# Two weight blocks tile by tile at the end of six stages, part of the norm's squares added on GpSimd, and one ring start moved

## The chip, the core and the metric

The kernel runs on one core of a Trainium2 chip. The metric is the device time of one execution in microseconds (us), the median of several runs. TensorE (PE in the rows; its weight loads are PEld) multiplies, VectorE is DVE, ScalarE is ACT, GpSimd is POOL, and SP is the engine whose queue issues most of the DMAs.

## What is computed

A residual stream x of 256 tokens by 1024 features goes through ten sublayers and a last norm. Each sublayer s is

```
h = rmsnorm(x) * g * (1 + scale_s) + shift_s        # over the 1024 features
x = x + gate_s * sublayer_s(h)
```

Sublayers 0, 2, 3 and 5 are dense (swiglu, 2816 wide: `silu(h @ w_gate) * (h @ w_up) @ w_down`), 1 is an SSD mixer, 4 an MLA attention, 6 and 8 are RWKV and pooling mixers, and 7 and 9 are a PEER layer: 128 * 128 experts, for each expert an input row u and an output row v, `sum over chosen e of gate_e * gelu(h . u_e) * v_e`, computed densely with a gate matrix that is zero where an expert isn't chosen. All in float32; each shift, scale and gate comes from a product of a condition with a modulation matrix.

## The kernel before

x lies in SBUF as 8 tiles (features on partitions) of 128 x 256 tokens. All weights come as 957 blocks of 128 x 1024 floats (512 KB), numbered in the order of use (`BASE` gives a stage's first block), through a ring of slots. `ring_plan` gives every block a slot; `CYCLES[first block] = (at, cycle)` says at which place `at` of which cycle of slots a stage starts. The dense stages use `WIDE`, 12 slots; the mixers behind them use only 4. `BEFORE[n]` is the block that had n's slot before. SP's queue issues the loads strictly in order, and waits ahead of each load until `BEFORE[n]` has been used (semaphore `block_used`, counted by TensorE).

A float32 product is made of three fast ones. For each block ScalarE writes a rounded copy into one of four places (`split_hi`, L1227, `weights_hi`; it waits for the load and until the block four back is used) and VectorE the rest in the block's own slot (`split_lo`, L1745). TensorE then runs for each of 8 tiles three matmuls (w hi by h hi, w hi by h lo, w lo by h hi): 24 matmuls a block. In the first parts of a stage (`columns_in_parts`, L590) one block makes one output tile; in the last part of the stages 0, 2, 3, 5, 7 and 9 (`rows_in_parts`, L622, "row stages") one block adds to all 8 output tiles, which lie in the four PSUM banks `acc`, two to a bank. There the second operand is a gate tile, made by ScalarE (`gate_hi`) and VectorE (`gate_lo`) a block or two ahead, and in the last block `acc_done` tells VectorE after tiles 1, 3 and 5 that a pair is complete.

Between two stages:

- VectorE, `residual` (L1737): `split_lo` of the next stage's first block, eight updates of x, `split_lo` of the second
- ScalarE, `norm_squares` (L1211): behind `split_hi` of the next two blocks (three where the stage is in `EARLY`: 1, 3, 4, 6), eight squares into `SQ`; then, when TensorE is ready, the square root (L1213)
- TensorE, `norm_sum` (L556): for each of 8 tiles 2 matmuls with a tile of ones, which the trace shows as 4; it sums over partitions. In `norm_spread` (L566) the root is spread; `open_acc` (L577) puts zeros in the four banks
- VectorE, `normed`: in an `EARLY` stage `split_lo` of the third block, then the root's refinement (L1705 to L1708), eight normed tiles (L1718); in the other stages `split_lo` of the third block now; then the low parts of h (L1752), and the fourth block
- ScalarE, `shift` (L1219): the high parts of h, each behind a normed tile; in stages not in `EARLY` the third `split_hi` comes ahead of it
- TensorE, `front` (L601, L602, L615): the high parts of two blocks paced by `shift`, the third block, and then the products with the low parts of h; the first block is released (`block_used`) in the middle of L615

GpSimd has its own order, one queue: DMAs of modulation weights (`mod_loads`, which wait for x of the stage and for VectorE's products) and of constants, and some adds inside stages 6 and 8.

Of the kernel before, what the change touches and what calls it, by code (L numbers as in the profile page):

```python
# [98 lines left out]
def uv_cycle(l):  # L99
# [5 lines left out]
          BASE["ffn", 1]: (1, WIDE), BASE["ffn", 2]: (0, WIDE), BASE["mla_in"]: (2, range(RING)), BASE["ffn", 3]: (1, WIDE),  # L105
# [131 lines left out]
EARLY = (1, 3, 4, 6)  # L237
BY_ROWS = (0, 2, 3, 5, 7, 9)
COND_ROWS = {0: 1, 1: 2, 3: 3}
# [25 lines left out]
def _consts():  # L265
# [13 lines left out]
    "norm_sq", "norm_pe", "mla_var", "norm_sqrt", "norm_dve", "h_ready", "x_upd",  # L279
# [7 lines left out]
    "rw_w", "rw_zpad", "rw_zeroed", "rw_shift", "rw_lora", "rw_vres", "rw_vresa", "rw_v", "rw_act", "rw_dve",  # L287
# [10 lines left out]
def build(nc, stream, mods, cols_d, consts_d, x_d, pos_d, wuq_d, wukv_d, cond_d, keys_d, pool_d, lora_d, gup_d, vup_d, acts_d, out_d):  # L298
    with ExitStack() as ctx:
# [50 lines left out]
        SQ = AR[:, 120:128, :]  # L350

# [194 lines left out]
        def _(pe):  # L546
# [5 lines left out]
            def norm_sum(s):  # L552
                for d in range(DT):
                    pe.wait_ge(sem["norm_sq"], 8 * s + d + 1)
                    for tt in range(TT):
                        mm = pe.matmul(PS[:, 2, tt * P:(tt + 1) * P], SQ[:, d, tt * P:(tt + 1) * P], ones, start=d == 0 and tt == 0,  # L556
                                       stop=d == DT - 1, skip_group_check=True)
                mm.then_inc(sem["norm_pe"], 1)
# [59 lines left out]
            def rows_in_parts(w, wl, hi, lo, last=False):  # L618

                for d in range(DT):  # L620
                    for lhs, rhs in ((w, hi), (w, lo), (wl, hi)):
                        mm = pe.matmul(acc[:, d, :], lhs[:, d, :], rhs, start=False, stop=False, skip_group_check=True)  # L622
                    if last and d in (1, 3, 5):
                        mm.then_inc(sem["acc_done"], 1)
                mm.then_inc(sem["block_used"], 1)
# [265 lines left out]
            def rwkv(l):  # L891
# [153 lines left out]
                pe.wait_ge(sem["rw_zeroed"], l + 1)  # L1045
# [62 lines left out]
            def peer(l):  # L1108
# [44 lines left out]
                open_acc()  # L1153

                def value(k, i, last=False):
                    w, wl = parts(v0 + k, i)
                    pe.wait_ge(sem["gate_lo"], i * UV_RING + (GATES["uv", l] + k + 1))
                    rows_in_parts(w, wl, gat_hi[:, k % 4, :], gat_lo[:, k % 4, :], last)

                for k in range(UV_RING):  # L1160
                    value(k, 0)
                pe.wait_ge(sem["pe_gelu"], NK * (l + 1))
                rephase(3)
                with pe.Fori(0, NK // UV_RING - 2) as i:
                    for k in range(UV_RING, 2 * UV_RING):
                        value(k, i)
                for k in range(UV_RING, 2 * UV_RING):
# [1344 lines left out]
```

## Time and profile before

| | us |
|---|---|
| median of 3 runs | 3295.07 |
| lowest, highest | 3293.87, 3315.15 |
| profiled execution | 3303.25 |
| its span | 3301.5 |
| PE busy in the span | 3180.2 (96%) |
| VectorE busy | 2521.2 (76%) |
| ScalarE busy | 1603.3 (49%) |
| GpSimd busy | 197.1 (6%) |

Times in rows are us from the span's start. Matmuls are pipelined: one is shown as about 0.28 long while the next starts 0.113 later. A duration with a count behind it (x8) is that of the whole group from first start to last end. `[0.78 <-PE psum L622]` means that the engine was idle 0.78 us ahead of it and what ended the wait.

### The profile page before, as it was taken

How to read it: one execution, taken by the hardware profiler on the slowest of the kernel's cores; microseconds unless marked ns; L12 is line 12 of the kernel's file. 1: busy time of each engine (PE TensorE's matmuls, PEld its weight loads, DVE VectorE, ACT ScalarE, POOL GpSimd, SP SyncE). 2: the span in 40 equal slices, each digit the busy share in tenths (PEclk: the TensorE clock that was granted, in tenths of full speed). 3: DMA queues.
4: the chain of work that ended last, by engine and by line, in shares of the span. 5: the costliest groups of instructions: out<-in, count | busy, mean ns of one | idle time of the engine just before them, and what ended most of it. 6: DMA issues, size and time to landing. Idle time of an engine off the chain costs nothing.

```text
span 3301.5 us, 71408 instructions
## 1 busy us (share of the span) xinstructions
PE 3180.2 (96%) x28256; PEld 3061.2 (93%) x28256; DVE 2521.2 (76%) x4560; ACT 1603.3 (49%) x2581; POOL 197.1 (6%) x331
## 2 busy tenths in 40 slices
PE   6999989999999999899999999999899999999998
PEld 6999769999967998889999999998789999999998
DVE  7989657989835896748978877776756978867776
ACT  4466644454544445335455454444425455554444
POOL 1100001111100110200000000000400000000000
PEclk9999999999999999999999999999899999999999
DMA  9965218979721993146875477774226885567774
GB/s 394 382 234 167 77 39 317 387 293 387 278 83 51 402 363 119 47 164 211 241 216 170 145 262 235 236 234 156 84 98 196 243 234 174 174 210 235 236 234 161
DMA packets 246741, 707.37 MB, mean 214 GB/s; under 512 B 27488, under 2 KB 93024, under 8 KB 245456
## 3 DMA queue, kind: packets, MB, share of 16 engines
q1 hardware_dynamic: 212256, 572.17, 52.0%
q0 software_dynamic: 34224, 131.55, 10.5%
q8 instruction: 185, 3.03, 0.4%
q14 instruction: 76, 0.62, 0.1%
HBM read 669.00 MB, written 34.60 MB: 213 GB/s over the span
## 4 chain that ended last, share of the span: by engine, by line
PE 89%; DVE 5%; DMA 3%; ACT 2%; issue 1%; SPq 0%; POOL 0%; DVEq 0%; ACTq 0%; POOLq 0%
PE psum L590 40%; PE psum L622 29%; PE psum L1149 3%; PE psum L1081 1%; PE psum L721 1%; DMA ring<-stream 1%; PE psum L973 1%; PE psum L556 1%; PE psum L996 1%; PE psum L769 1%; PE psum L601 1%; DVE ring L1745 1%; PE psum L602 1%; PE psum L888 1%; DVE arena L1803 1%
## 5 line engine op out<-in xcount | busy, mean ns | idle before, releaser
L590 PE MATMUL psum<-hh,weights_hi 128*128 128x256 f32 x4216 | 1186.7, 281 | 19.2 <-ACT arena L1444 8.8
L590 PE MATMUL psum<-h,weights_hi 128*128 128x256 f32 x4216 | 1171.6, 278 | 0.0
L590 PEld LDWEIGHTS psum<-hh,weights_hi 128*128 128x128 f32 x4216 | 798.0, 189 | 25.5 <-issue 11.3
L590 PEld LDWEIGHTS psum<-h,weights_hi 128*128 128x128 f32 x4216 | 797.4, 189 | 0.2
L622 PE MATMUL psum<-small,weights_hi 128*128 128x256 f32 x2752 | 768.1, 279 | 4.5 <-DVE ring L1745 3.9
L622 PE MATMUL psum<-work,weights_hi 128*128 128x256 f32 x2752 | 766.5, 279 | 0.0
L1745 DVE TENSOR_TENSOR ring<-ring,weights_hi 128x1024 fp32r<-128x1024 f32 x463 | 566.0, 1225 | 181.7 <-ACT weights_hi L1227 176.9
L1227 ACT ACTIVATE weights_hi<-ring 128x1024 fp32r<-128x1024 f32 x463 | 488.2, 1056 | 374.0 <-PE psum L622 182.0
L590 PE MATMUL psum<-hh,ring 128*128 128x256 f32 x2016 | 562.4, 279 | 0.0
L622 PEld LDWEIGHTS psum<-small,weights_hi 128*128 128x128 f32 x2752 | 519.4, 189 | 5.5 <-DVE ring L1745 5.4
L622 PEld LDWEIGHTS psum<-work,weights_hi 128*128 128x128 f32 x2752 | 519.0, 189 | 0.0
L1227 ACT ACTIVATE weights_hi<-arena 128x1024 fp32r<-128x1024 f32 x334 | 351.5, 1053 | 100.0 <-PE psum L590 78.7
L590 PEld LDWEIGHTS psum<-hh,ring 128*128 128x128 f32 x2016 | 383.2, 190 | 0.0
L622 PE MATMUL psum<-small,ring 128*128 128x256 f32 x1280 | 354.0, 277 | 0.0
L590 PE MATMUL psum<-hh,more_lo 128*128 128x256 f32 x1240 | 343.7, 277 | 0.0
L1745 DVE TENSOR_TENSOR more_lo<-arena,weights_hi 128x1024 fp32r<-128x1024 f32 x214 | 261.1, 1222 | 52.7 <-ACT weights_hi L1227 48.6
L1657 DVE SCALAR_TENSOR_TENSOR arena<-arena 128x1024 f32<-128x1024 f32 x232 | 282.2, 1219 | 17.8 <-DMA arena<-stream 12.6
L2216 DVE TENSOR_TENSOR work<-work,arena 128x256 f32<-128x256 f32 x256 | 163.8, 641 | 164.7 <-PE psum L622 164.2
L622 PE MATMUL psum<-small,v_lo 128*128 128x256 f32 x1024 | 289.2, 282 | 0.0
L1566 ACT ACTIVATE small<-psum 128x256 f32<-128x256 f32 x256 | 97.9, 383 | 381.7 <-PE psum L590 376.1
L590 PE MATMUL psum<-hh,u_lo 128*128 128x256 f32 x960 | 265.2, 276 | 0.0
L622 PEld LDWEIGHTS psum<-small,ring 128*128 128x128 f32 x1280 | 240.3, 188 | 0.0
(420 smaller groups left out, 4901.9 us busy)
## 6 DMA issues: line engine op xcount, KB each, us to landing
ring<-stream SPq DMA_DIRECT2D x487, 512.0 KB, 4.2
arena<-stream SPq DMA_DIRECT2D x342, 512.0 KB, 5.2
arena<-mod_weights POOLq DMA_DIRECT2D x224, 512.0 KB, 7.1
v_raw<-stream SPq DMA_DIRECT2D x128, 512.0 KB, 4.4
acts<-small SPq DMA_DIRECT2D x256, 128.0 KB, 3.6
work<-acts SPq DMA_DIRECT2D x256, 128.0 KB, 3.2
arena<-w_uq POOLq DMA_DIRECT2D x1, 3072.0 KB, 10.6
arena<-cond_rows POOLq DMA_DIRECT2D x2, 1024.0 KB, 8.4
```

The lines of the kernel that those rows point to most:

```text
L556: mm = pe.matmul(PS[:, 2, tt * P:(tt + 1) * P], SQ[:, d, tt * P:(tt + 1) * P], ones, start=d == 0 and tt == 0, stop=d == DT - 1, skip_grou ...
L590: mm = pe.matmul(out, lhs[:, d, :], rhs[:, d, :], start=(d == 0 and p == 0), stop=(d == DT - 1 and p == 2))
L601: pe.matmul(out, w[:, d, :], h_hi[:, d, :], start=opens and d == 0, stop=False, skip_group_check=True)
L602: pe.matmul(out, wl[:, d, :], h_hi[:, d, :], start=False, stop=False, skip_group_check=True)
L622: mm = pe.matmul(acc[:, d, :], lhs[:, d, :], rhs, start=False, stop=False, skip_group_check=True)
L721: mm = pe.matmul(to, XTOK[:, tt, at], rhs, start=k == 0, stop=k == 3, skip_group_check=True)
L1149: mm = pe.matmul(PS[:, 4 + g % 4, j * P:(j + 1) * P], OHI[:, g % 2, j, :], OHJ[:, g % 2, j, :], start=True, stop=True)
L1227: act.activation(whi[:, NTH[n] % WS, :], raw(n), ACT.Copy).then_inc(sem["block_hi"], 1)
L1566: act.activation((rs, rv)[n % 2], PS[:, n % 4, 0:T], ACT.Gelu).then_inc(sem["pe_gelu"], 1)
L1657: return dve.scalar_tensor_tensor(PRODUCT[:, m % 2, :], block, 1.0, COND[:, 0 if g < 6 else 1, :], ALU.mult, ALU.mult, accum_out=modc[:, g ...
L1745: dve.tensor_tensor(low(n), raw(n), whi[:, NTH[n] % WS, :].bitcast(F32), ALU.subtract)\
L2216: dve.tensor_tensor(gat[:, k % 4, :], sil[:, k % 4, :], WALL[:, :, i * UV_RING + k], ALU.mult).then_inc(sem["pe_gated"], 1)
```

## The change

- `last_rows`: in a row stage TensorE runs the last two blocks together, tile by tile: 3 matmuls of the one and 3 of the other for tile 0, and so on. `acc_done` comes after tiles 1, 3, 5 and 6; both blocks are released at tile 7.
- Tile 7 of the row stages is accumulated in bank 0, `PS[:, 0, 0:T]`, opened by a matmul of zeros (`open_last`) behind the column part.
- In dense stages gate tiles use four places instead of two and are made one block further ahead.
- For s in 1, 3, 4, 6, 8 and the last norm GpSimd adds squares 0 to 3 into the place of square 3 (`norm_presum`), and TensorE sums tiles 4, 3, 5, 6, 7 only.
- `EARLY` is gone: in all stages the third block is split behind the squares.
- `CYCLES` of the dense stage 3 (blocks 213 to 278) starts at 6 instead of 0.
- `rw_zpad` is merged into `rw_zeroed`.

The diff, cut to its core:

```diff
-          BASE["ffn", 1]: (1, WIDE), BASE["ffn", 2]: (0, WIDE), BASE["mla_in"]: (2, range(RING)), BASE["ffn", 3]: (1, WIDE),
+          BASE["ffn", 1]: (1, WIDE), BASE["ffn", 2]: (6, WIDE), BASE["mla_in"]: (2, range(RING)), BASE["ffn", 3]: (1, WIDE),
...
-EARLY = (1, 3, 4, 6)
 BY_ROWS = (0, 2, 3, 5, 7, 9)
+PRE, PRESUMMED = 4, tuple(s + 1 for s in BY_ROWS)
...
+        def row_acc(d):
+            return acc[:, d, :] if d < DT - 1 else PS[:, 0, 0:T]
...
             def norm_sum(s):
-                for d in range(DT):
-                    pe.wait_ge(sem["norm_sq"], 8 * s + d + 1)
+                added = s in PRESUMMED
+                order = (PRE, PRE - 1, *range(PRE + 1, DT)) if added else range(DT)
+                for n, d in enumerate(order):
+                    if added and d == PRE - 1:
+                        pe.wait_ge(sem["norm_pre"], (PRE - 1) * (PRESUMMED.index(s) + 1))
+                    else:
+                        pe.wait_ge(sem["norm_sq"], 8 * s + d + 1)
...
+            def last_rows(blocks):
+
+                for d in range(DT):
+                    for block in blocks:
+                        mm = row_parts(d, *block)
+                        if d == DT - 1:
+                            mm.then_inc(sem["block_used"], 1)
+                    if d in (1, 3, 5, 6):
                         mm.then_inc(sem["acc_done"], 1)
+            def open_last():
+
+                pe.matmul(row_acc(DT - 1), zeros[:, :], rep(zeros[:, :], 2), start=True, stop=False, skip_group_check=True)
...
+                pe.wait_ge(sem["ffn_a"], FT * f + FT - 1)
+                open_last()
+                last = []
                 for j in range(FT):
                     w, wl = parts(base + 2 * FT + j)
                     pe.wait_ge(sem["gate_lo"], GATES["ffn", f] + j + 1)
-                    rows_in_parts(w, wl, gat_hi[:, j % 2, :], gat_lo[:, j % 4, :], j == FT - 1)
+                    if j < FT - 2:
+                        rows_in_parts(w, wl, gat_hi[:, j % 4, :], gat_lo[:, j % 4, :])
+                    else:
+                        last.append((w, wl, gat_hi[:, j % 4, :], gat_lo[:, j % 4, :]))
+                last_rows(last)
...
                 root_table((0, 2, 3, 5)[f] + 1)
-                for j in range(FT - 2):
+                gate_hi(2)
+                for j in range(FT - 3):
                     ready(base + 2 * FT + j)
-                    gate_hi(j + 2)
+                    gate_hi(j + 3)
...
-                    for p in range(3 if s in EARLY else 2):
+                    for p in range(2):
                         split_hi(FIRST[s] + p)
                 norm_squares(s)
-                if s and s not in EARLY:
+                if s:
                     split_hi(FIRST[s] + 2)
...
-                    if s in BY_ROWS and d < 6:
-                        dve.wait_ge(sem["acc_done"], 3 * BY_ROWS.index(s) + d // 2 + 1)
+                    if s in BY_ROWS and d < 7:
+                        dve.wait_ge(sem["acc_done"], 4 * BY_ROWS.index(s) + d // 2 + 1)
...
+            def norm_presum(s):
+
+                for d in range(1, PRE):
+                    pool.wait_ge(sem["norm_sq"], 8 * s + d + 1)
+                    if d > 1:
+                        pool.wait_ge(sem["norm_pre"], (PRE - 1) * PRESUMMED.index(s) + d - 1)
+                    pool.tensor_tensor(SQ[:, d, :], SQ[:, d - 1, :], SQ[:, d, :], ALU.add).then_inc(sem["norm_pre"], 1)
```

VectorE's gates in the dense stages are moved in the same way as ScalarE's, the PEER stages call `last_rows` for their last two blocks, and `norm_presum` stands in GpSimd's queue behind the modulation loads of the stage ahead (stages 1, 3, 4), ahead of the constants of stages 6 and 8, and at the end for the last norm.

## Rows read from the trace of the kernel before

**Rows 1.** The page, part 4: the chain that ended last, by line.

```profile
PE psum L590 40%; PE psum L622 29%; PE psum L1149 3%; PE psum L1081 1%; PE psum L721 1%; DMA ring<-stream 1%; PE psum L973 1%; PE psum L556 1%; PE psum L996 1%; PE psum L769 1%; PE psum L601 1%; DVE ring L1745 1%; PE psum L602 1%; PE psum L888 1%; DVE arena L1803 1%
```

**Rows 2.** Chain of stage 0's end (start us, us, what).

```profile
204.93 14.39 PE psum L622 x127
219.32 3.58 PE psum L556 x32
```

**Rows 3.** Timeline behind stage 0 (start, us, engine, line, tiles, count [idle <-releaser]).

```profile
217.32 3.23 DVE L1737 SCALAR_TENSOR_TENSOR x<-psum,modc,x 128x256 f32<-128x256 f32 x8 [0.78 <-PE psum L622]
217.84 3.16 ACT L1211 ACTIVATE arena<-x 128x256 f32<-128x256 f32 x8
...
222.62 0.64 PEld L577 LDWEIGHTS psum<-zeros 128*128 128x128 bf16 x4
222.93 0.26 ACT L1213 ACTIVATE small<-psum,eps 128x2 f32<-128x2 f32 x1 [1.93 <-PE psum L556]
224.78 3.22 DVE L1718 SCALAR_TENSOR_TENSOR h<-x,modc,psum 128x256 f32<-128x256 f32 x8 [0.81 <-PE psum L566]
...
232.52 0.47 ACT L1282 ACTIVATE arena<-psum,cols 128x256 f32<-128x256 f32 x1 [2.97 <-PE psum L615]
```

**Rows 4.** Timeline, stages 6 and 8: GpSimd adds and VectorE beside them.

```profile
1310.93 2.47 POOL L2320 TENSOR_TENSOR arena<-arena 128x1024 f32<-128x1024 f32 x1 [40.66 <-DVE arena L1981]
1311.19 2.48 DVE L1974 SCALAR_TENSOR_TENSOR arena<-arena,cols 128x256 f32<-128x256 f32 x1
1315.64 0.48 DVE L1974 SCALAR_TENSOR_TENSOR arena<-arena,cols 128x256 f32<-128x256 f32 x1
...
2371.05 0.73 POOL L2355 TENSOR_TENSOR small<-small,arena 128x256 f32<-128x256 f32 x1
2371.46 0.41 DVE L2023 TENSOR_TENSOR arena<-psum,arena 128x256 f32<-128x256 f32 x1
```

**Rows 5.** Timeline, ScalarE and VectorE behind stage 7.

```profile
2273.87 1.05 ACT L1227 ACTIVATE weights_hi<-ring 128x1024 fp32r<-128x1024 f32 x1
2275.56 3.22 DVE L1718 SCALAR_TENSOR_TENSOR h<-x,modc,psum 128x256 f32<-128x256 f32 x8 [0.81 <-PE psum L566]
2278.70 1.22 DVE L1745 TENSOR_TENSOR ring<-ring,weights_hi 128x1024 fp32r<-128x1024 f32 x1
...
2283.62 0.39 ACT L1444 ACTIVATE arena<-psum 128x256 f32<-128x256 f32 x1 [3.29 <-PE psum L615]
```

**Rows 6.** Timeline, TensorE behind stage 9.

```profile
3288.41 3.73 PE L556 MATMUL psum<-kept,arena 128*128 128x128 f32 x32
```

**Rows 7.** Chain from stage 3 into stage 4.

```profile
896.76 3.24 DVE x L1737 x8
...
904.49 12.32 DMA arena<-constants
```

**Rows 8.** Timeline in stage 8: SP issues a lone load, ScalarE takes it.

```profile
2283.55 13.88 SPq L536 DMA_DIRECT2D ring<-stream  x6
...
2286.89 1.06 ACT L1227 ACTIVATE weights_hi<-ring 128x1024 fp32r<-128x1024 f32 x1 [2.88 <-DMA ring<-stream]
```

**Rows 9.** The page, part 6 (queue, operation, count, KB each, us to landing).

```profile
ring<-stream SPq DMA_DIRECT2D x487, 512.0 KB, 4.2
```

**Rows 10.** Chain behind stage 2.

```profile
711.95 3.58 PE psum L556 x32
715.56 0.27 ACT small L1213
```

**Rows 11.** TensorE by stretch (us, busy (x count), granted clock, DMA share, GB/s).

```profile
376.00:378.00 2.00, 0.00 (x0) 1.00 0.70 236
378.00:380.00 2.00, 0.00 (x0) 0.62 0.07 27
...
386.00:388.00 2.00, 2.00 (x7) 0.50 0.00 0
388.00:390.00 2.00, 2.00 (x11) 0.82 0.00 0
```

More of the change, by code:

```diff
@@ L552, in norm_sum @@
             def norm_sum(s):
[L553 to L554 removed]
+                added = s in PRESUMMED
[5 more added lines that the diff above has]
+                        pe.wait_ge(sem["norm_sq"], 8 * s + d + 1)
                     for tt in range(TT):
[L556 removed]
+                        mm = pe.matmul(PS[:, 2, tt * P:(tt + 1) * P], SQ[:, d, tt * P:(tt + 1) * P], ones, start=n == 0 and tt == 0,
                                        stop=d == DT - 1, skip_group_check=True)
@@ L616, in front, with row_parts, rows_in_parts @@
                     mm.then_inc(sem["block_used"], 1)
-            def rows_in_parts(w, wl, hi, lo, last=False):
-                for d in range(DT):
-                    for lhs, rhs in ((w, hi), (w, lo), (wl, hi)):
-                        mm = pe.matmul(acc[:, d, :], lhs[:, d, :], rhs, start=False, stop=False, skip_group_check=True)
-                    if last and d in (1, 3, 5):
+            def row_parts(d, w, wl, hi, lo):
+                for lhs, rhs in ((w, hi), (w, lo), (wl, hi)):
+                    mm = pe.matmul(row_acc(d), lhs[:, d, :], rhs, start=False, stop=False, skip_group_check=True)
+                return mm
+            def rows_in_parts(w, wl, hi, lo):
+                for d in range(DT):
+                    mm = row_parts(d, w, wl, hi, lo)
+                mm.then_inc(sem["block_used"], 1)
[4 more added lines that the diff above has]
+                        if d == DT - 1:
+                            mm.then_inc(sem["block_used"], 1)
+                    if d in (1, 3, 5, 6):
                         mm.then_inc(sem["acc_done"], 1)
-                mm.then_inc(sem["block_used"], 1)
+            def open_last():
+                pe.matmul(row_acc(DT - 1), zeros[:, :], rep(zeros[:, :], 2), start=True, stop=False, skip_group_check=True)
             def ffn(s, f):
@@ L1165, in peer @@
                     for k in range(UV_RING, 2 * UV_RING):
-                        value(k, i)
-                for k in range(UV_RING, 2 * UV_RING):
-                    value(k, NK // UV_RING - 2, k == 2 * UV_RING - 1)
+                        rows_in_parts(*value(k, i))
+                for k in range(UV_RING, 2 * UV_RING - 2):
+                    rows_in_parts(*value(k, NK // UV_RING - 2))
+                last_rows([value(k, NK // UV_RING - 2) for k in (2 * UV_RING - 2, 2 * UV_RING - 1)])
             def begin(s):
@@ L1720, in normed @@
                 if s in IN_PARTS:
-                    if s and s not in EARLY:
+                    if s:
                         split_lo(FIRST[s] + 2)
@@ L1784, in ffn @@
                         products(2 * k + 1)
-                for j in range(FT - 2):
-                    gate_lo(j + 2)
-                    if j + 4 + 2 * FT < 3 * FT:
+                gate_lo(2)
+                for j in range(FT - 3):
+                    gate_lo(j + 3)
+                    if j + 4 < FT:
                         split_lo(base + 2 * FT + j + 4)
```

37 lines of the change are left out of this document (21 added, 16 removed).

## The prediction

> **What bounds the kernel now.** I read the page first, its chain of work that ended last [rows 1]: two lines, both TensorE's streams of 24 matmuls for one weight block, hold 69% of the span. So the kernel is a train of matmuls, and what the change can touch is what stands between two trains: the norm ahead of each stage. Next I read the chain at the end of stage 0 [rows 2]: 127 matmuls in 14.39 us (0.113 each) run up to 219.32, and then the 32 matmuls of the norm's sum take 3.58 us (0.112 each) without a gap. ScalarE and VectorE beside them [rows 3]: the eight residual updates run from 217.32 to 220.55 (first to last 0.396 apart, each 0.48), the eight squares from 217.84 to 221.00. The last square is done before TensorE comes to it at about 222.3, so it is TensorE, not the residual, that decides when the square root starts (222.93). What the reader is to see: the residual is late but not on the path; the norm's sum is.
>
> **What is added up and left out of the sum.** Four tiles of squares become one. TensorE then does 5 tiles of 4 matmuls instead of 8, so 12 fewer, 12 x 0.112 = 1.34 us per transition [rows 2]. Conditions: the last square and the GpSimd sum must be there. With two blocks interleaved, the train of 48 matmuls starts at 219.32 - 48 x 0.113 - 0.17 = 213.7, and a pair of accumulators is done every 1.36 us, more than the 0.79 us that two residuals take. So only tile 7 is left at the end: residual at 219.36 to 219.84, square to 220.3 [rows 3], ahead of its turn on TensorE (219.3 + 16 x 0.112 = 221.1). GpSimd: tiles 2 and 3 are updated at about 217.5, the square of 3 is there at 217.95. An add of this shape takes 0.73 us [rows 4], and the third ends at about 219.1, some 0.6 us before TensorE has done with tile 4. Hidden, with little to spare.
>
> An add beside VectorE needs a look [rows 4]. A GpSimd add of 2.47 us stretched a VectorE instruction with both inputs in SBUF from the 0.48 us that it takes at 1315.64 to 2.48 us, till after the add had ended (1313.40); an instruction with one input in PSUM kept its 0.41 us beside another add. The residuals read PSUM, so they should keep their time; the split of the second weight block (1.2 us, both inputs in SBUF) starts at 219.85, after the adds. The cost is taken as 0; bounds 0 and one add (0.7 us) per transition. By the Trainium skill, GPSIMD Engine Reference, section Specifications, GpSimd's interfaces to SBUF are shared with VectorE and contend with its instructions that have two SBUF inputs. The trace agrees (2.48 beside 0.48); if that rule bit at each transition it would be the third rival below.
>
> **The split of the third weight block moves.** For stages 1, 3, 4 and 6 it moves from ahead of the squares to behind the square root on ScalarE, and on VectorE from ahead of the root to behind the eight normed tiles. It has to: its place in weights_hi is held by the last block but one, now in use up to the end. The kernel already has this order in stage 8 [rows 5]: ScalarE's 1.05 us (2273.87 to 2274.92) ends before the first normed tile is there (2276.04), free; VectorE's 1.2 us pushes the low parts of h. From the start of the normed tiles to the first evacuation it takes 2283.62 - 2275.56 = 8.06 us there, and 232.52 - 224.78 = 7.74 in stage 1 [rows 3]. So +0.32 us in each of the four. The matmul wait for the low parts is where it sits.
>
> **Stage by stage.** Into stage 1: -1.34 + 0.32 = -1.02. Into 6: the same, -1.02 (the fourth block behind it is fetched by a load that starts when the first is released, so it moves along). Into 8: -1.34, no split moved. Into the last norm: -1.34; the sum follows the matmuls there too, 3.73 us for the 32 [rows 6]. Into stage 4 the chain is another [rows 7]: eight residuals, then GpSimd issues loads that wait for them, and the DMA of 12.32 us up to 916.81 holds the stage. TensorE's gain is lost in that wait; what counts is when the last residual ends, 220.55 - 219.84 = 0.71 us earlier as worked out for stage 0. So -0.71. The turned ring also brings this stage's first loads earlier, but they are not on this path. Sum of the five: -5.43.
>
> The extra matmul that opens the eighth accumulator: four of twice its width load in 0.64 us [rows 3], so about 0.1 us each, six times, on TensorE's path: +0.6. Its waits (for a gate product or gelu two or more blocks back) are over by then; bounds 0 and 1.2. The two gate tiles that must be ready one block sooner are covered by making the third one ahead of the loop; the waits behind which they queue are for block j, as before. On GpSimd the adds are queued ahead of loads that wait for the whole of x, which comes after them, so they delay nothing, but in stage 3 perhaps 0.4 us. The merged semaphore costs nothing.
>
> **The ring that was turned.** This is the edit that I would watch. The stage ahead (147 to 212, starting at 1) leaves its last block, 212, in slot (1 + 65) mod 12 = 6. Starting stage 3 at 6 puts its *first* block, 213, in slot 6 as well. SP's queue therefore waits for block 212 to be used before it may load 213, and all later loads queue behind it. Before, the block ahead in that slot was seven blocks back. After 212 is used, in order: the load, ScalarE's rounding, VectorE's low part, and only then the residuals, because both engines have this split queued ahead of the residual and the squares. Prices: a load with nothing else in flight took 2286.89 - 2283.55 = 3.34 us until ScalarE had it [rows 8]; the median over all loads of this kind is 4.2 [rows 9]. The train of stage 2 ends at 711.95 and the square root behind it is at 715.56 [rows 10]. In the new kernel:
> - 711.95 + 0.1 + 3.34 = 715.4 landed; rounding 1.05, 716.45; low part 1.2, 717.7
> - eight residuals 3.23, 720.95; last square 721.4; third add about 721.35
> - TensorE does tile 4 at 720.3, then 16 matmuls from 721.4. At 0.112 that is 1.8 us and the square root starts at 723.4, +7.8 us.
>
> But TensorE has then been idle from 711.95 to 720.3. In a gap that has no matmul from 376 to 380 the granted clock fell from 1.00 (0.62 is a mean over a stretch of both levels); it was 0.50 at 386 to 388, with TensorE at work again, and came back between 388 and 390 [rows 11]. 0.50 is the lower of its two levels, 1.2 against 2.4 GHz. At double the time the 16 matmuls take 3.6 us: +9.6, the value that I take, since the gap here is twice as long as those 4 us. By the Trainium skill, TensorE: Matmul & The Clock Gate, section What's actually happening, the gate knows only these two rates and falls to the lower one when the engine idles. The trace agrees (1.00, 0.50); at the high rate the stage would cost 7.8. With 0.3 for the moved split: +9.9. Bounds: 8.1 (clock kept) and 12.5 (a load of 4.2 us, and a further 1.7 us for matmuls of the front at the lower clock).
>
> **Sum.** -5.4 + 0.6 + 9.9 = +5.1 us on a profiled execution of 3303.25 us (span 3301.5). That one is 8.2 above the median of the runs, 3295.07. The difference carries over: 3295.07 + 5.1 = 3300.2.
>
> **Rivals.**
> - *The turned ring costs nothing* (the load is hidden in some way that I don't see). For it: loads are early in most of the span. Against it: one in-order queue and a wait on block 212. Then -5.4 + 0.6 + 0.3 - 1.34 = -5.8, 3289.2, faster. It decides if the load of 213 is issued before the last matmul of 212. Chance 0.10.
> - *The stall is dearer*: twelve loads are now issued at one go, the first lands at 4.2 us or later, and the half clock lasts into the front. +2.6 to +5: 3303 to 3305. Chance 0.20.
> - *The adds come too late or hold VectorE up.* If the third add ends 1.3 us after 219.1, or two adds hold VectorE's split, each of five transitions loses what it gained: 5.4 less gain, 3305.6. For it: the margin is 0.6 us and [rows 4]. Against: PSUM operands escape. Chance 0.10.
> - Something that I haven't seen makes it slower by over 33 us: 0.02; faster by as much: 0.01.
>
> **How the numbers follow.** The forecast has 0.57, with its own range 3297 to 3303 (the bounds of the stall and of the opening matmul). The range that holds the time 8 times in 10 reaches from the first rival to beyond the third: 3290 to 3307. One per cent is 33 us, about what a measurement of this kernel can tell from no change. All cases but the last lie within it: faster 0.01, same 0.97, slower 0.02.
>
> **What the profile would show.** Right: 20 matmuls of the norm's sum instead of 32 at six transitions, square root 1.3 us after where the train would put it; last residual alone at the end of a row stage; the first evacuation 8.06 us behind the first normed tile everywhere; behind block 212 TensorE idle for about 8 us with ScalarE's wait put down to the DMA of the ring, and a granted clock of 0.50 there. Wrong: a gap of less than 5 us at stage 3; a wait of TensorE on GpSimd in the norm's sum; residuals longer than 0.48 us; or a gain into stage 4 of more than 0.7, if its loads were held up by those that the turned ring moves.

## The result and the profile after

| us | before | after |
|---|---|---|
| median of 20 runs each | 3297.38 | 3309.32 |
| lowest, highest | 3291.95, 3315.15 | 3300.72, 3319.83 |
| profiled execution | 3303.25 | 3304.77 |
| its span | 3301.5 | 3303.1 |

Time after over time before is 1.0031, with a 95% interval of 1.002 to 1.0041: 10.2 us slower (6.6 to 13.5). That is within 1%, as forecast, and on the side that was forecast, but 3309.32 lies 9.1 us above the forecast of 3300.2 and 2.3 above the range. (Each of the kernels e5 and h1 below has one run far from all others, at 8143.96 and 5934.33 us, which neither its median nor its ratio takes in.)

The page of the kernel after: its head, and the chain that ended last by line.

```profile
span 3303.1 us, 71272 instructions
PE 3170.0 (96%) x28190; PEld 3048.8 (92%) x28190; DVE 2520.3 (76%) x4560; ACT 1603.9 (49%) x2581; POOL 212.3 (6%) x349
...
PE psum L599 39%; PE psum L630 29%; PE psum L1182 3%; PE psum L1114 1%; PE psum L754 1%; DMA ring<-stream 1%; PE psum L1006 1%; PE psum L1029 1%; PE psum L610 1%; PE psum L565 1%; PE psum L802 1%; DVE ring L1780 1%; PE psum L611 1%; DVE arena L1839 1%; PE psum L838 1%
```

The two trains hold 68% of the span (L599 and L630 are what L590 and L622 were in [rows 1]). GpSimd has 15 us more to do: 18 adds. Line numbers have moved, so here is the key: L630 is the row train, L565 the norm's sum, L586 the zeros, L575 the spread, L1263 and L1780 the two splits of a weight block, L1247 the squares, L1249 the square root, L1753 the normed tiles, L1772 the residual, L2309 the new GpSimd adds, L540 SP's load.

**The end of stage 0**, chain (start, us, what) and then timeline of the kernel after, to be laid beside [rows 2, 3]:

```profile
204.89 14.85 PE psum L630 x131
219.74 2.24 PE psum L565 x20
222.01 0.27 ACT small L1249
```

```profile
218.42 1.84 DVE L1772 SCALAR_TENSOR_TENSOR x<-psum,modc,x 128x256 f32<-128x256 f32 x4 [0.48 <-PE psum L630]
218.07 1.62 POOL L2309 TENSOR_TENSOR arena<-arena 128x256 f32<-128x256 f32 x2 [0.23 <-ACT arena L1247]
223.86 3.22 DVE L1753 SCALAR_TENSOR_TENSOR h<-x,modc,psum 128x256 f32<-128x256 f32 x8 [0.81 <-PE psum L575]
231.86 0.48 ACT L1319 ACTIVATE arena<-psum,cols 128x256 f32<-128x256 f32 x1 [3.23 <-PE psum L624]
```

What the reader is to see: 20 matmuls in 2.24 us where there were 32 in 3.58, without a gap; GpSimd is done at 219.69, before TensorE comes to the sum's second tile, the one that holds the adds' result (the two rows of VectorE and GpSimd are the last four of eight updates and the last two of three adds). From the last matmul of the train to the first normed tile it takes 223.86 - 219.74 = 4.12 us, and 224.78 - 219.32 = 5.46 before: exactly the 1.34 us forecast.

**The end of stage 2**, chain of the kernel after, to be laid beside [rows 10]:

```profile
699.89 10.55 PE psum L630 x93
710.46 3.55 DMA arena<-stream
714.04 1.06 ACT weights_hi L1263
715.13 1.23 DVE more_lo L1780
716.35 0.41 DVE x L1772
716.78 0.82 ACT arena L1247 x2
717.67 0.73 POOL arena L2309
718.54 0.74 POOL arena L2309
719.40 1.80 POOL arena L2309
721.25 3.80 PE psum L565 x16
725.08 0.27 ACT small L1249
```

Here the train is over at 710.44 and TensorE waits. The load of block 213 starts when block 212 is released, and behind it stand, one after the other, the two splits, one residual, two squares, the adds. Between the train's end and the first normed tile (726.92) lie 16.49 us, where it was 5.46.

The same distance for all kernels below is the table that the rest rests on; what each kernel is follows in the next section. The last column is stage 4 whole, from the last matmul of stage 3's train to the last of stage 4's. Into stages 2, 5, 7 and 9 it is 5.46 in all kernels (once 5.79).

| last matmul to first normed tile, us, into | 1 | 3 | 4 | 6 | 8 | last norm | stage 4 whole |
|---|---|---|---|---|---|---|---|
| before | 5.46 | 5.46 | 6.48 | 5.46 | 5.46 | 5.46 | 170.8 |
| before, a second profile (b1) | 5.46 | 5.46 | 6.57 | 5.46 | 5.46 | 5.46 | 171.1 |
| after | 4.12 | 16.49 | 4.11 | 4.12 | 4.11 | 4.12 | 170.8 |
| after again (e0) | 4.12 | 16.29 | 4.12 | 4.12 | 4.12 | 4.12 | 171.0 |
| after, ring start 0 (e1) | 4.11 | 4.12 | 8.45 | 4.12 | 4.12 | 4.12 | 172.2 |
| before, ring start 6 (e2) | 5.46 | 15.32 | 5.46 | 5.46 | 5.45 | 5.46 | 171.3 |
| after, ring start 2 (e3) | 4.12 | 4.12 | 4.12 | 4.12 | 4.12 | 4.12 | 171.3 |
| e3 again (e4) | 4.12 | 4.12 | 4.11 | 4.12 | 4.12 | 4.12 | 170.2 |
| e3 a third time (e5) | 4.12 | 4.11 | 4.11 | 4.12 | 4.11 | 4.11 | 171.3 |
| e3 without the adds (f1) | 5.46 | 5.46 | 5.46 | 5.46 | 5.45 | 5.46 | 170.1 |
| e3, blocks in turn (f2) | 6.93 | 6.93 | 8.05 | 8.05 | 8.32 | 5.78 | 172.6 |
| e3, one bank less (f3) | 4.12 | 4.12 | 4.12 | 4.12 | 4.12 | 4.12 | 172.3 |
| after, splits behind squares (g1) | 4.12 | 7.24 | 4.12 | 4.12 | 4.12 | 4.12 | 171.1 |
| e3, positions apart (h1) | 4.12 | 4.12 | 4.12 | 4.12 | 4.12 | 4.12 | 168.3 |

### The profile page after: what moved, and what is told of

Its sections match the earlier page's. It is cut to its first block, busy times and chain, and to the rows that moved or that the text cites. A ratio compares the mean times of both kernels' runs of the same rounds, so it can differ in the third digit from the quotient of the medians.

```text
span 3303.1 us, 71272 instructions
## 1 busy us (share of the span) xinstructions
PE 3170.0 (96%) x28190; PEld 3048.8 (92%) x28190; DVE 2520.3 (76%) x4560; ACT 1603.9 (49%) x2581; POOL 212.3 (6%) x349
## 3 DMA queue, kind: packets, MB, share of 16 engines
q0 software_dynamic: 34224, 131.55, 10.4%
## 4 chain that ended last, share of the span: by engine, by line
PE 88%; DVE 5%; DMA 3%; ACT 2%; issue 2%; SPq 0%; POOL 0%; DVEq 0%; ACTq 0%; POOLq 0%
PE psum L599 39%; PE psum L630 29%; PE psum L1182 3%; PE psum L1114 1%; PE psum L754 1%; DMA ring<-stream 1%; PE psum L1006 1%; PE psum L1029 1%; PE psum L610 1%; PE psum L565 1%; PE psum L802 1%; DVE ring L1780 1%; PE psum L611 1%; DVE arena L1839 1%; PE psum L838 1%
## 5 line engine op out<-in xcount | busy, mean ns | idle before, releaser
L599 PE MATMUL psum<-hh,weights_hi 128*128 128x256 f32 x4216 | 1187.4, 282 | 21.9 <-DVE ring L1780 8.9
L599 PE MATMUL psum<-h,weights_hi 128*128 128x256 f32 x4216 | 1171.5, 278 | 0.0
L599 PEld LDWEIGHTS psum<-hh,weights_hi 128*128 128x128 f32 x4216 | 797.0, 189 | 28.9 <-issue 11.7
L599 PEld LDWEIGHTS psum<-h,weights_hi 128*128 128x128 f32 x4216 | 797.6, 189 | 0.3
L630 PE MATMUL psum<-small,weights_hi 128*128 128x256 f32 x2752 | 768.1, 279 | 4.6 <-DVE ring L1780 3.6
L630 PE MATMUL psum<-work,weights_hi 128*128 128x256 f32 x2752 | 766.4, 278 | 0.0
L1780 DVE TENSOR_TENSOR ring<-ring,weights_hi 128x1024 fp32r<-128x1024 f32 x459 | 561.5, 1225 | 179.1 <-ACT weights_hi L1263 175.0
L1263 ACT ACTIVATE weights_hi<-ring 128x1024 fp32r<-128x1024 f32 x459 | 484.5, 1056 | 378.4 <-PE psum L630 184.7
L599 PE MATMUL psum<-hh,ring 128*128 128x256 f32 x2024 | 564.3, 279 | 0.0
L630 PEld LDWEIGHTS psum<-small,weights_hi 128*128 128x128 f32 x2752 | 518.9, 189 | 5.7 <-DVE ring L1780 5.7
L630 PEld LDWEIGHTS psum<-work,weights_hi 128*128 128x128 f32 x2752 | 519.0, 189 | 0.0
L1263 ACT ACTIVATE weights_hi<-arena 128x1024 fp32r<-128x1024 f32 x338 | 355.9, 1054 | 109.4 <-PE psum L599 77.0
L599 PEld LDWEIGHTS psum<-hh,ring 128*128 128x128 f32 x2024 | 384.5, 190 | 0.0
L630 PE MATMUL psum<-small,ring 128*128 128x256 f32 x1264 | 349.6, 277 | 0.0
L599 PE MATMUL psum<-hh,more_lo 128*128 128x256 f32 x1232 | 341.2, 277 | 0.0
L1780 DVE TENSOR_TENSOR more_lo<-arena,weights_hi 128x1024 fp32r<-128x1024 f32 x218 | 266.2, 1223 | 59.0 <-ACT weights_hi L1263 55.6
L630 PE MATMUL psum<-small,v_lo 128*128 128x256 f32 x1024 | 289.3, 283 | 0.0
L599 PE MATMUL psum<-hh,u_lo 128*128 128x256 f32 x960 | 265.5, 277 | 0.0
L630 PEld LDWEIGHTS psum<-small,ring 128*128 128x128 f32 x1264 | 237.3, 188 | 0.0
```

Source lines behind the costliest of these rows:

```text
L599: mm = pe.matmul(out, lhs[:, d, :], rhs[:, d, :], start=(d == 0 and p == 0), stop=(d == DT - 1 and p == 2))
L630: mm = pe.matmul(row_acc(d), lhs[:, d, :], rhs, start=False, stop=False, skip_group_check=True)
L1263: act.activation(whi[:, NTH[n] % WS, :], raw(n), ACT.Copy).then_inc(sem["block_hi"], 1)
L1780: dve.tensor_tensor(low(n), raw(n), whi[:, NTH[n] % WS, :].bitcast(F32), ALU.subtract)\
```

## The experiments

Times are medians of 11 to 13 runs. The kernels were measured in four groups, each on one chip with the kernel before beside it, and only kernels of one group are compared: e0 to e3; e4 and f1 to f3; e5, g1 and h1; b1. The ratio is not that of the two medians and can differ from it by some us (2.5 at most).

| | this | before | ratio (95%) |
|---|---|---|---|
| e0_after_again | 3309.99 | 3299.45 | 1.0032 (1.0018 to 1.0046) |
| e1_ring_back | 3298.38 | 3299.45 | 0.9998 (0.9985 to 1.0011) |
| e2_ring_alone | 3312.85 | 3299.45 | 1.0033 (1.002 to 1.0046) |
| e3_ring_two | 3298.57 | 3299.45 | 0.9993 (0.998 to 1.0005) |
| e4_ring_two_again | 3305.44 | 3310.61 | 0.9977 (0.9956 to 0.9997) |
| f1_no_presum | 3308.37 | 3310.61 | 0.9989 (0.9969 to 1.0008) |
| f2_blocks_in_turn | 3321.38 | 3310.61 | 1.0022 (1.0003 to 1.0042) |
| f3_shared_bank | 3308.21 | 3310.61 | 0.998 (0.996 to 1.0) |
| e5_ring_two_third | 3294.95 | 3297.69 | 0.9999 (0.9987 to 1.0011) |
| g1_splits_behind | 3301.17 | 3297.69 | 1.001 (1.0 to 1.0021) |
| h1_positions_apart | 3292.27 | 3297.69 | 0.9977 (0.9962 to 0.9991) |
| b1_before_itself | 3301.25 | 3298.35 | 1.0006 (0.9994 to 1.0019) |

### Is it the ring? (e0, e1, e2, e3)

e0 is the changed kernel once more, for comparison with the others.

> The changed kernel as it is, for a second profile beside the others on one chip. Theory (the turned ring costs a stall ahead of stage 3, the rest gains): square root of stage 3 again 14.5 us or more behind the end of the train of stage 2 instead of 3.6, and 2.27 instead of 3.61 at the five other transitions. Rival (a loss outside the transitions, in the gates or in the queue of GpSimd): the stage bodies, from the first normed tile of a stage to the end of its last train, are longer than before by 5 us in all. Time: 8 to 12 us above the kernel before on either.

e1 is the changed kernel with the old ring start:

```diff
-          BASE["ffn", 1]: (1, WIDE), BASE["ffn", 2]: (6, WIDE), ...
+          BASE["ffn", 1]: (1, WIDE), BASE["ffn", 2]: (0, WIDE), ...
```

> The changed kernel with stage 3's ring starting at 0 again. Theory: the whole loss is the load of block 213; without it the square root of stage 3 is 2.3 us behind its train, the kernel is 12 to 15 us faster than the changed one and 4 to 6 us faster than the kernel before. Stage 4 gives back about 1 us, since its first loads are late again. Rival (loss outside the transitions): the time stays 0 to 5 us above the kernel before.

e2 is the kernel before with nothing but the new start:

```diff
-          BASE["ffn", 1]: (1, WIDE), BASE["ffn", 2]: (0, WIDE), ...
+          BASE["ffn", 1]: (1, WIDE), BASE["ffn", 2]: (6, WIDE), ...
```

> The kernel before with stage 3's ring starting at 6 and nothing else. Theory: 11 to 15 us slower than the kernel before; three splits instead of two are queued ahead of the squares, so the stall is a little longer than in the changed kernel (square root 15 to 17 us behind the train). Rival: 5 us slower or less, the other 5 to 10 us of the changed kernel coming from its other edits.

e3 is the changed kernel with a start that gives neither stage an early block in a slot that is in use to the end: 213 comes into the slot of 208, five blocks back (that of 212 goes to the fifth block, 217), and stage 4's first two blocks into those of 273 and 274:

```diff
-          BASE["ffn", 1]: (1, WIDE), BASE["ffn", 2]: (6, WIDE), ...
+          BASE["ffn", 1]: (1, WIDE), BASE["ffn", 2]: (2, WIDE), ...
```

> The changed kernel with stage 3's ring starting at 2: the first block of stage 3 takes the place of the fifth block before it, and stage 4's first blocks those of the sixth and fifth. Theory: no stall at either place, square root 2.3 us behind the train in both, 4 to 7 us faster than the kernel before, the fastest of the four by 0 to 2 us. Rival: as for the ring put back, 0 to 5 us above the kernel before.

Measured: with the start at 6 both orders of work are about 11 us slower than before (e0 +10.5, e2 +10.9), and with it at 0 or 2 neither is (e1 -0.7, e3 -2.3, both with zero inside their interval). e0 - e1 is 11.6 us, e0 - e3 11.4. The stall is 16.29 in e0 and 15.32 in e2, against 4.12 and 5.46. So the turned ring alone makes the whole loss, and this is shown from both sides: added alone to before, and taken back alone from after. Two expectations missed. The stall of e2 was to be longer than that of the changed kernel and is 1 us shorter: it has no adds in its chain. And e1 and e3 were to be 4 to 7 us faster than before; their transitions are, but their times don't show it.

e1 also shows what a start of 0 costs together with the rest of the change. Stage 4's second block, 280, then lies in the slot of 276. Chain of e1 into stage 4:

```profile
893.37 3.21 DMA ring<-stream
...
896.60 1.06 ACT weights_hi L1263
897.67 2.46 ACT arena L1247 x8
900.12 1.50 POOL arena L2309
```

The same place in the timeline, VectorE's split of the second block:

```profile
899.37 1.67 DVE L1780 TENSOR_TENSOR ring<-ring,weights_hi 128x1024 fp32r<-128x1024 f32 x1
```

The last two blocks together hold TensorE up to 898.8, but the load could start only at 893.37, when 276 was released; ScalarE rounds at 896.60 and its squares, which could have begun with the first residuals at 896.24, stand behind that. 8.45 us instead of 4.12 is the price at this place. Part of it is that the adds and VectorE's split now meet: the split took 1.67 us instead of 1.22 beside the second add, and the third add 1.5 instead of 0.73 beside the split. Against the new order of work, then, start 0 loses 4.3 us into stage 4 and start 6 loses 12.2 us into stage 3; start 2 loses neither. But stage 4 as a whole is only 0.9 us longer in e1 than in e3 (172.2 and 171.3), and about 1 was expected: the chain of e1 goes on through the wait for GpSimd's loads, shown below with h1, and these land 19.9 us behind the train in e1 and 19.1 in e3. The turn avoids a wait that is there (before had a bit of it: 6.48), and buys a larger one.

### Which part gains? (e4, f1, f2, f3)

e4 is e3 once more. f1, f2 and f3 each take one part out of it.

> Stage 3's ring at 2 once more, as the base of the three beside it. Every norm behind a row stage starts its first normed tile 4.12 us behind the train (5.46 before), stage 4's 4.12 (6.48 before). Theory (all effects of the change are those seen at the transitions): 5 to 8 us faster than the kernel before. Rival (something that the transitions don't show takes it back): 0 to 3 us faster.

f1: no adds, TensorE sums all eight tiles:

```diff
-PRE, PRESUMMED = 4, tuple(s + 1 for s in BY_ROWS)
+PRE, PRESUMMED = 4, ()
...
-                for d in range(1, PRE):
+                for d in range(0):
```

> Ring at 2, without GpSimd's adds: TensorE sums all eight tiles of squares. Theory: 5.46 instead of 4.12 us from train to normed tile at stages 1, 3, 6, 8 and the last norm, and stage 4 unchanged in its end (its loads hold it), so 5 x 1.34 = 6.7 us slower than the base. Rival (the adds hold VectorE up elsewhere, or upset the queue of GpSimd): stage bodies get shorter without them, and the time stays within 3 us of the base.

f2: the last two blocks one after the other, as in before:

```diff
+                rows_in_parts(*blocks[0])
                 for d in range(DT):
-                    for block in blocks:
-                        mm = row_parts(d, *block)
-                        if d == DT - 1:
-                            mm.then_inc(sem["block_used"], 1)
+                    mm = row_parts(d, *blocks[1])
                     if d in (1, 3, 5, 6):
                         mm.then_inc(sem["acc_done"], 1)
+                mm.then_inc(sem["block_used"], 1)
```

> Ring at 2, with the last two blocks one after the other again (tile by tile only in the last one; accumulator 7 keeps its own bank). Theory: the residual then ends 0.7 us later and its pairs come 0.68 us apart, so the square of tile 3 is 0.1 to 0.3 us behind the train and the third add 1.6 to 2 us behind it: TensorE waits for the add after tile 4, and the step from train to normed tile takes 5.2 to 5.6 us. All of the 1.34 us is gone: 6 to 7 us slower than the base. Rival (the adds alone bring the gain): 4.1 to 4.4 us per step, within 2 us of the base.

f3: the eighth accumulator back in the bank of the seventh, with `acc_done` after tiles 1, 3 and 5 as before:

```diff
-            return acc[:, d, :] if d < DT - 1 else PS[:, 0, 0:T]
+            return acc[:, d, :]
...
-                pe.matmul(row_acc(DT - 1), zeros[:, :], rep(zeros[:, :], 2), start=True, stop=False, skip_group_check=True)
+                pass
```

> Ring at 2, accumulator 7 back beside 6 in one bank, no opening matmul, the last pair updated together behind the train. Theory: the last square is ready 1.4 us behind the train, TensorE wants it 1.8 us behind it, so the bank of its own brings nothing: step 4.1 us, the opening matmuls save 0.6 us, within 1 us of the base. Rival: the later square shows, step 4.5 us, 2 us slower.

Measured: f1 has 5.46 everywhere, so the 1.34 us is the adds' and theirs alone. In the medians f1 is 2.9 us above e4, which the intervals (some 6 us either way) tell neither from 0 nor from the 6.7 that the traces give. f3 is 2.8 above e4 with the same 4.12 everywhere: the bank of its own bought nothing that can be seen, neither in the trace nor in the time. f2 is the one with something to say: 15.9 us slower than e4. Timeline of f2 behind stage 2:

```profile
712.76 3.52 POOL L2308 TENSOR_TENSOR arena<-arena 128x256 f32<-128x256 f32 x3 [26.84 <-ACT arena L1246]
714.49 1.21 DVE L1779 TENSOR_TENSOR ring<-ring,weights_hi 128x1024 fp32r<-128x1024 f32 x1
713.90 0.71 PE L565 MATMUL psum<-kept,arena 128*128 128x128 f32 x4 [0.55 <-ACT arena L1246]
716.33 2.05 PE L565 MATMUL psum<-kept,arena 128*128 128x128 f32 x16 [1.72 <-POOL arena L2308]
```

Without the two blocks together, the residuals begin as late as in before, the third add falls on VectorE's split of the second block (714.49), and TensorE waits 1.72 us for GpSimd with 16 matmuls still to do. The third add took 714.51 to 716.29, 1.78 us; the two ahead of it 0.74 each. At the last norm no weight block is split, and there, in the same kernel, the third add took 0.73 us. Six transitions of 5.78 to 8.32 us are the result, all worse than the 5.46 without any adds (5.2 to 5.6 was expected; that had left this contention out). Into stages 4, 6 and 8 they are the longest because part of the 16 matmuls then ran at a granted clock of 0.50 (into stage 8 they took 3.55 us instead of 2.07). So the adds pay only with the two last blocks run together, which makes squares 0 to 3 early; the two edits are one.

### What the stall is made of (g1, e5)

g1 is the changed kernel, ring start 6 included, but at stage 3 ScalarE rounds the first two blocks behind the squares, and VectorE makes their low parts behind the root instead of around the residual:

```diff
-                if s and s in IN_PARTS:
+                if s and s in IN_PARTS and s != 3:
                     for p in range(2):
                         split_hi(FIRST[s] + p)
                 norm_squares(s)
+                if s == 3:
+                    for p in range(2):
+                        split_hi(FIRST[s] + p)
```

> The changed kernel with the late load left as it is (ring at 6), but at stage 3 the splits of its first two blocks moved: ScalarE rounds them behind the squares, VectorE makes their low parts behind the refined root instead of around the residual. Theory (the load alone is 3.5 us; it costs 11 to 12 us because residual, squares and adds queue behind the two splits): residual, squares and norm's sum run at once, while the load is under way; the square root comes behind ScalarE's two splits, 5.8 to 6.2 us behind the train, VectorE's splits end about 9 us behind it. Train to first normed tile 8.5 to 9.5 us instead of 16.4, 7 to 8 us faster than the changed kernel, 2 to 4 us slower than the kernel before. Rival (the load's own time and the half clock are the cost, whatever the order): 14 us or more.

Beside it in its group stands e3's kernel for the third time:

> Ring at 2 as base of the two beside it: 5 to 8 us faster than the kernel before by its transitions; 2 to 8 by the two earlier measurements of it.

Chain of g1 into stage 3:

```profile
699.99 13.73 PE psum L630 x121
713.73 0.33 SPq L540
714.11 0.43 SPq L540
714.58 7.10 DMA arena<-stream
721.70 1.06 ACT weights_hi L1263
722.76 0.41 ACT hh L1255
723.21 0.58 PE psum L610
723.79 0.21 PE psum L611
```

Into stage 3 it now takes 7.24 us (8.5 to 9.5 expected) instead of 16.49, and the front 13.34 instead of 9.6: 3.1 and 3.7 us above e3, 6.8 in all where the changed kernel has 12.3. The medians say the same: g1 is 6.2 us above e5 in its group, e0 11.4 above e3 in its own. So about half of the stall is not the load itself: it is that residual, squares and adds stood behind two splits which the load held back, on two engines that take their work in order. What is left in g1 is another load of the same burst, the third to be issued, which took 7.10 us to land, and a front at half clock (matmuls 0.21 apart instead of 0.12).

### Where the gain into stage 4 went (h1)

h1 is e3 with one small load taken out of GpSimd's queue. The angles that VectorE makes first in stage 4 need only the positions, but the wait is for all four of GpSimd's loads. SP issues the positions, on another semaphore, and TensorE's wait for the other three counts to 48:

```diff
+                if n == BASE["mla_in"] + RING:
+                    sp.wait_ge(sem["x_upd"], 32)
+                    sp.dma_start(ANG[:, 0, :].bitcast(I32), pos_d[0:1, :].to_broadcast([64, T])).then_inc(sem["first_cond"], 16)
...
-                dve.wait_ge(sem["mla_w"], 64)
+                dve.wait_ge(sem["first_cond"], 32)
...
-            pool.dma_start(ANG[:, 0, :].bitcast(I32), pos_d[0:1, :].to_broadcast([64, T])).then_inc(sem["mla_w"], 16)
```

> Ring at 2, and in stage 4 the positions are loaded by SP on a semaphore of their own, so VectorE's angles no longer wait for 5 MB of other constants on GpSimd's queue. Theory (stage 4 is held by that wait, which swallowed the gain of its norm): from the end of stage 3's train to the end of stage 4's train 2 to 5 us less than the 170.2 to 171.4 of the other kernels; 2 to 5 us faster than the base, the fastest kernel of all. Rival (the ring's loads are as late as the constants, so another wait of the same length follows): within 1 us of the base there.

Chain of the kernel after into stage 4, to be laid beside [rows 7], and that of h1:

```profile
908.74 0.50 DVE x L1772
...
909.52 0.55 POOL arena L2348
...
913.74 13.92 DMA arena<-constants
```

```profile
898.88 2.24 PE psum L568 x20
...
910.99 7.13 DMA ring<-stream
918.14 1.06 ACT weights_hi L1266
919.23 1.24 DVE ring L1783
920.51 9.51 PE psum L602 x61
```

In the kernel after, the transition itself gained (4.11 instead of 6.48), and stage 4 as a whole nothing (170.8 and 170.8): VectorE waits for the constants, which land at 927.66. That wait was there before too, but from the last issue to landing it took 12.32 us [rows 7] and takes 13.92 now. In h1 it is gone from the chain, the next wait there is a load of the ring, and stage 4 takes 168.3 us, 1.9 to 3.0 less than in the three profiles of e3's kernel. The time agrees: the median is 2.7 us under that of e5 in its group (the ratios of the two would make it 7), and by its ratio h1 is 7.6 us (3.0 to 12.5) faster than before. The interval of e4 leaves out 1 too, but those of e3 and e5, the same kernel, don't.

### The kernel before against itself (b1)

> The kernel before against itself, to see how much of a few us is measurement, and for a second profile of it. With no hidden effect the ratio is 1 within 0.0015 (5 us). If the kernels with the new transitions have a loss outside them, as their times (2 to 3 us less gain than their transitions give) might say, then the bodies of stages 7 and 9 in this profile are near the 811 to 814 of the first one, while those kernels have 811 to 819; if it is drift, this profile lies anywhere in 811 to 819.

The ratio is 1.0006 with 1 inside its interval. What b1 adds is a second profile of before. TensorE in stage 5, by stretch, in the profile of before and then in that of b1 (stretch, length, busy (x matmuls), granted clock, DMA share, GB/s):

```profile
1120.00:1140.00 20.00, 20.00 (x172) 1.00 1.01 394
1140.00:1160.00 20.00, 20.00 (x172) 1.00 1.02 397
```

```profile
1120.00:1140.00 20.00, 20.00 (x179) 1.00 1.03 408
1140.00:1160.00 20.00, 20.00 (x179) 1.00 1.02 400
```

The same instructions at the same granted clock, 172 in 20 us in the one and 179 in the other. Stage 5's train took 179.8 us in the one and 173.9 in the other. In b1 it is stage 2 that is slow, 179.7 instead of 173.9. In 8 of the 14 profiles some dense stage is 3 to 6 us long in this way, and not always the same one.

It is not a gradual drift: in the dense stages 72 matmuls in a row take 8.16 us or 8.48, and a train keeps one pace for long stretches (stage 5 of before has the slow one from its first quarter to its end, that of e1 to two thirds). Stage 7 of e4, 6.9 us longer than that of before, has 62 more runs of 24 matmuls at the slow pace (2.83 us instead of 2.72). What sets the pace is open.

As to the question asked: the trains of stages 7 and 9 took 814.0 and 812.9 us in b1, 811.3 and 813.7 in the first profile of before, and 810.8 to 819.0 in the kernels with the new transitions. That is what was expected with a hidden loss, but a scatter from one execution to the next can give it too: 17 of the 22 values of those kernels lie between 810.8 and 814.9. So b1 decides nothing here.

## Why the prediction was right and wrong

**Right, and by its own steps.** The mechanism of each part was as forecast. Into stage 1 the sum has 20 matmuls and the gain is 1.34; the same 1.34 into 6, 8 and the last norm. The residuals keep their time beside the adds (3.22 us for eight at 716.27, [rows 3] 3.23). The moved split costs 231.86 - 223.86 = 8.00 us from normed tile to evacuation, where 7.74 was measured and 8.06 forecast. The turned ring costs what it was said to cost, in the way that it was said: SP's wait for block 212, the load, both splits, then the residual; TensorE idle from 710.44 to 718.82, and half the clock. TensorE by stretch in the kernel after:

```profile
711.00:713.00 2.00, 0.00 (x0) 1.00 0.79 242
713.00:715.00 2.00, 0.00 (x0) 0.94 1.02 408
715.00:717.00 2.00, 0.00 (x0) 0.50 1.03 412
...
723.00:725.00 2.00, 2.00 (x11) 0.50 1.00 399
```

0.50 is the lower of its two levels. The 16 matmuls at the end of the sum took 3.80 us at it (3.6 forecast, 1.8 at 0.112 each). The rival in which the ring costs nothing is refuted by e2, and the one that the adds are too late or hold VectorE up by the 4.12 at every transition but the one at stage 3. The rival of a dearer stall came true in size but not by its causes: the load took 3.55 us, and the clock was back before the front.

**Wrong: the stall was mis-sized, 9.6 forecast and 11.0 measured at the square root.** The step is "third add about 721.35", in the list for stage 3. With the train's end 1.5 us earlier that is 719.85; it ended at 721.20. All steps ahead of it came within 0.3 us: landed 714.04 (forecast 713.9), low part done 716.36 (716.2), tile 4's matmuls at 718.82 (718.8). The reason stands in the timeline of the kernel after:

```profile
717.67 3.53 POOL L2309 TENSOR_TENSOR arena<-arena 128x256 f32<-128x256 f32 x3 [34.68 <-ACT arena L1247]
719.40 1.22 DVE L1780 TENSOR_TENSOR more_lo<-arena,weights_hi 128x1024 fp32r<-128x1024 f32 x1
721.25 3.79 PE L565 MATMUL psum<-kept,arena 128*128 128x128 f32 x16 [1.21 <-POOL arena L2309]
```

Both start at 719.40, the third add and VectorE's split of the second block, whose inputs both lie in SBUF. The add took 1.80 us instead of 0.73, and TensorE waited 1.21 us for it. The prediction looked at just this pair for stage 0, where the adds are over 0.5 us before the split, and priced contention at 0 for all; at stage 3, where its own list lets the adds run up to the moment at which the split begins, it was not asked again. It had named a wait of TensorE on GpSimd in the norm's sum as a sign of being wrong, and here it is. Nor is it always VectorE that pays. In [rows 4] the GpSimd add began 0.26 us ahead and VectorE's instruction was stretched; here VectorE's instruction kept its 1.22 us and the add was stretched by 1.1; in f2, where VectorE began 0.02 us ahead, the same (1.78); in e1 the add began 0.14 us ahead, kept its 0.73, and the split took 1.67. Where one clearly began first, that one ran on, and the other ended after it. The Trainium skill, GPSIMD Engine Reference, section Specifications, names the pair (contention where VectorE's instruction has two SBUF inputs); the trace agrees (1.80 instead of 0.73).

**Wrong: -0.71 into stage 4.** Measured 0 (170.8 and 170.8; 171.0 in e0). That the gain would be lost in the wait for the constants was right; that their landing would come earlier with the last residual was not. They landed 927.66 - 909.24 = 18.4 us after it instead of 916.81 - 900.00 = 16.8. SP's queue in the kernel before and in the one after:

```profile
912.98 4.86 SPq L536 DMA_DIRECT2D ring<-stream  x4
```

```profile
920.80 5.04 SPq L540 DMA_DIRECT2D ring<-stream  x4
```

These four loads are released by stage 4's front and begin 8.5 us after the last constants were issued in before (904.49) and 7.1 us in after (913.74). The shorter norm brings them 1.4 us nearer, and the constants land 1.6 us later. That the one causes the other is argued from these numbers and from a DMA share of about 1 at that place; no run moved those loads alone. The other profiles bear it out where GpSimd's four issues lie 4.2 us apart, first to last, as here. The earlier the ring's loads begin after the last issue, the longer it takes to land: 8.4 to 8.6 us behind it, 12.3 us (before, b1, f1); 7.5, 12.9 (e2); 7.1, 13.7 to 14.1 (after, e0, e3, e4, e5, g1); 6.7, 14.5 (f3). In e1 and f2 the issues lie closer together, and the rule fails (10.4 and 10.2; 13.9 in both). What h1 shows is that the wait is where the gain stops.

**The opening matmul** was taken at +0.6; the trains of stages 0 and 3 grew from 171.99 to 172.14 us in the profiles without a slow stretch, 0.15 each, and in f3, which leaves the matmul out, that of stage 0 took 172.01. Six times 0.15 is +0.9 (the other four stages have no such clean pair): as good as right.

**How 3300.2 became 3309.3.** The terms that can be seen in the profiles sum to: stall +11.0, four transitions -5.4, moved split and fronts +0.7, opening matmuls +0.9, stage 4 0: +7.2 instead of +5.1. That is 2.1 of the 9.1, and 1.4 of it is the stretched add. Another 2.3 is the starting point: the median of before is 3297.38 over 20 runs and was 3295.07 over 3. With these two the forecast would have been 3304.6, inside the range. The ratio says +10.2 (6.6 to 13.5), so 3.0 us are in no term, and the two medians stand 11.9 apart, another 1.7. The 3.0 lie within the interval, and the other kernels don't agree on them: against before, e1 has -0.7 measured and about -4 by the terms, e3 -2.3 and e5 -0.3 where the terms give about -5, but e4, the same kernel, -7.6; h1 has -7.6 and about -8; f1 -3.6 and about +1. The four kernels of e4's group all lie 2 to 5 us under their terms, and those of e0's group with the new transitions about 3 above, so the gap goes with the group of runs as much as with the kernel. Whether some three microseconds are lost in the long stages, where the profiles scatter by more than that from one execution to the next, or whether it is chance, stays open. So of the steps of the prediction two are known to be wrong, the price of the add beside the split (0 taken, 1.1 us measured) and the earlier end of stage 4's wait (0.71 taken, 0 measured), and neither alone, nor both, carries the time out of the range.

The two profiled executions stand only 1.6 us apart, and would have supported "no change". Before's has the slow stage 5, 5.8 us that have nothing to do with the kernel. And the range was too narrow on the upper side for a plain reason: it took in the unknown costs, but not that a median of three runs with 21 us between lowest and highest is itself known to a few us only.

## What to carry to other kernels

Where slots are given out over a stage border, count for every block of the next stage how long its slot is in use, in the order in which TensorE will really release the blocks; running two blocks together moves both releases to the end. A load of 3.6 us cost 12; 5.5 of them were gone when residual, squares and adds no longer stood in order behind its splits: what doesn't need the load should stand ahead of what does. Adds given to an idle engine pay only if their operands are early; ask at each place, not at one, whether they meet an instruction of VectorE with two SBUF inputs.

## What the runs showed of the hardware

- GpSimd's add of 128 x 256 takes 0.73 to 0.74 us alone, and 1.78 to 1.80 when it meets a VectorE instruction of 1.22 us with two SBUF inputs that begins with it or 0.02 us ahead, and that keeps its time. Where the add began 0.14 us ahead it kept 0.73, and the VectorE instruction took 1.67 (e1).
- The first load of 512 KB behind a released slot reached its consumer after 3.2 us (e1), 3.6 (after) and 3.8 (g1); the third of g1's burst took 7.10.
- TensorE had no matmul from 710.44 to 718.82; the granted clock was 0.50 in the stretches from 715 to 725, the 16 matmuls of the sum took 3.80 us, and it was 1.00 again from 725.
- A whole dense stage can run at 172 matmuls per 20 us instead of 179 at a granted clock of 1.00: 5.8 us of 174. There are two paces, 72 matmuls in 8.16 or in 8.48 us.
